# Thirteen small vector loads issued by SyncE behind the first weights, instead of by ScalarE

## What is computed

```python
hn = rmsnorm(h, norm_mix_g[l])      # h is x, (1, 512, 1024)
proj = hn @ w_in[l]                 # (1024, 3592), taken 256 columns at a time
fq, fk, fv, ff, gq, gf, gi, gg = jnp.split(proj, split_idx, axis=-1)
```

## Time and profile before

| | |
|---|---|
| median of 3 runs | 2095.19 us (2094.62 to 2097.42) |
| the profiled execution | 2095.3 us, its span 2093.5 us |
| busy share of the span | PE 97%, VectorE 57%, GpSimd 43%, ScalarE 36% |
| chain that ended last | PE 87%, VectorE 5%, issue 3%, ScalarE 2%, GpSimd 2%, DMA 1% |
| first transpose of x on PE | 5.02 us |
| first matmul of unit 0 | 18.69 us |
| mean granted clock of TensorE | 0.992 |

### The profile page before, as it was taken

How to read it: one execution, slowest core, us unless ns; L and a number is a source line. 1 busy time by engine, 2 the same in 40 slices (tenths; PEclk the granted TensorE clock), 3 DMA queues, 4 the chain that set the end, 5 groups by cost and what they waited for, 6 DMA issues and landing times.

```text
span 2093.5 us, 26082 instructions
## 1 busy us (share of the span) xinstructions
PE 2040.7 (97%) x10286; PEld 1698.6 (81%) x10286; DVE 1197.1 (57%) x1950; ACT 748.8 (36%) x1023; POOL 890.7 (43%) x488
## 2 busy tenths in 40 slices
PE   7999899999999999998999999999999899999998
PEld 6878787888888888876788888888898788888887
DVE  5454656546878895677688766616775763111112
ACT  5344424333513223445643222124353343222221
POOL 3322424654444444444334443443454334444442
PEclk9999999999999999999999999999999999999999
DMA  4322203514455543230146555323332022233321
GB/s 143 106 88 75 76 1 100 159 64 149 137 184 194 179 162 100 81 130 27 41 161 201 174 169 200 119 81 103 101 121 74 31 81 90 96 97 101 101 90 71
DMA packets 225198, 233.39 MB, mean 111 GB/s; under 512 B 4259, under 2 KB 220148, under 8 KB 224956
## 3 DMA queue, kind: packets, MB, share of 16 engines
q1 hardware_dynamic: 224704, 231.70, 34.0%
q10 hardware_dynamic: 380, 0.11, 0.0%
HBM read 229.55 MB, written 2.24 MB: 111 GB/s over the span
## 4 chain that ended last, share of the span: by engine, by line
PE 87%; DVE 5%; issue 3%; ACT 2%; POOL 2%; DMA 1%; ACTq 0%; DVEq 0%; POOLq 0%
PE ps L2329 21%; PE ps L2331 21%; PE ps L2330 21%; PE ps L2380 7%; PE ps L2385 3%; POOL wL L619 2%; PE ps L3156 1%; PE ps L3170 1%; PE ps L2842 1%; DMA raw<-in_w_xkv_dram 1%; PE ps L2773 1%; PE ps L2623 1%; PE ps L2803 1%; DVE ssum L1403 1%; DVE adacc L1866 1%
## 5 line engine op out<-in xcount | busy, mean ns | idle before, releaser
L619 POOL TENSOR_TENSOR wL<-raw,wH 128x1024 fp32r<-128x1024 f32 (+2 forms) x322 | 774.3, 2426 | 1029.5 <-ACT wH L781 969.5
L781 ACT ACTIVATE wH<-raw 128x2048 fp32r<-128x2048 f32 (+2 forms) x161 | 302.4, 1878 | 441.7 <-PE ps L2331 323.9
L2329 PE MATMUL ps<-uH,wH 128*128 128x512 f32 x1088 | 428.2, 394 | 4.7 <-DVE uL L1452 1.9
L2331 PE MATMUL ps<-uH,wL 128*128 128x512 f32 x1088 | 424.7, 390 | 0.0
L2330 PE MATMUL ps<-uL,wH 128*128 128x512 f32 x1088 | 424.1, 390 | 0.0
L2329 PE MATMUL ps<-hnH,wH 128*128 128x512 f32 x728 | 288.8, 397 | 0.0
L2331 PE MATMUL ps<-hnH,wL 128*128 128x512 f32 x728 | 284.1, 390 | 0.0
L2330 PE MATMUL ps<-hnL,wH 128*128 128x512 f32 x728 | 283.4, 389 | 0.0
L1866 DVE SCALAR_TENSOR_TENSOR adacc<-adaw,small,adacc 128x256 f32<-128x256 f32 x336 | 273.5, 814 | 12.0
L2329 PEld LDWEIGHTS ps<-uH,wH 128*128 128x128 f32 x1088 | 204.8, 188 | 49.8 <-issue 4.6
L2331 PEld LDWEIGHTS ps<-uH,wL 128*128 128x128 f32 x1088 | 204.7, 188 | 43.4
(11 more groups left out here) (461 smaller groups left out, 3109.9 us busy)
## 6 DMA issues: line engine op xcount, KB each, us to landing
raw<-in_ffn_w_dram SPq DMA_DIRECT2D x60, 1024.0 KB, 5.3
adaw<-in_ada_w_dram SPq DMA_DIRECT2D x48, 1024.0 KB, 7.3
raw<-in_w_dram SPq DMA_DIRECT2D x32, 1024.0 KB, 5.3
raw<-in_w_in_dram SPq DMA_DIRECT2D x14, 1024.0 KB, 5.4
raw<-in_od_w_in_dram SPq DMA_DIRECT2D x12, 1024.0 KB, 5.3
raw<-in_w_xkv_dram SPq DMA_DIRECT2D x8, 1024.0 KB, 5.7
raw<-in_ffn_w_dram SPq DMA_DIRECT2D x8, 768.0 KB, 4.3
raw<-in_ev_w_in_dram SPq DMA_DIRECT2D x5, 1024.0 KB, 5.2
```

The source lines that it names most:

```text
L619: nc.gpsimd.tensor_tensor(wL[n % 2][:, k0:k1, 0:c], raw[n % 2][:, k0:k1, 0:c], wH[n % 2][:, k0:k1, 0:c].bitcast(F32), ALU.subtract).then_i ...
L781: nc.scalar.activation(wH[n % 2][:, 0:kc, 0:c], raw[n % 2][:, 0:kc, 0:c], ACT.Copy).then_inc(w_hi, 1)
L2329: nc.tensor.matmul(out_ap, wh, xh, start=first, stop=False)
L2331: return nc.tensor.matmul(out_ap, wl, xh, start=False, stop=last)
```

## The change

The first six vector loads (mix, x, memory, feed-forward and final gains, and the lower-bound logits) stay on ScalarE. The other 13 (six rows of the table, four halves of the q and k gains, `ada_b`, `fox_f_bias`, `od_gate_b`) are issued by SyncE, after unit 0 and ahead of the two constant loads and of unit 1. Sources, destinations and the semaphore are the same, and PE waits for all 19 as before. The table of names moved out of ScalarE's program, and the loop's body became `load_vector`.

```diff
+    VECTORS = [("norm_mix_g", V_MIX, 8), ("norm_x_g", V_X, 8), ("norm_mem_g", V_MEM, 8), ("norm_ff_g", V_FF, 8),
+               ("final_norm_g", V_FINAL, 8), ("hgrn_lb_logits", V_LB, 8), ("hgrn_norm_g", V_HG, 1),
+               ("c_2", V_C, 8),
+               ("ev_b_pool_2", V_BPOOL, 4), ("ev_pool_scale_2", V_SPOOL, 4), ("od_conv_w_2", V_CW, 40),
+               ("od_conv_b_2", V_CB, 8)]
+
+    def load_vector(engine, row):
+        name, r0, count = row
+        src = a[name]
+        nd = len(src.shape)
+        flat = {1: "a -> a", 2: "a b -> (a b)", 3: "a b c -> (a b c)"}[nd]
+        src = src if nd == 1 else src.rearrange(flat)
+        return engine.dma_start(vrow[r0:r0 + count, :], src.rearrange("(r m) -> r m", m=P))
@@ -498,6 +512,14 @@
                 sp.dma_start(xtok[:, tb, :], a["x"][0, tb * P:(tb + 1) * P, :]).then_inc(x_in[tb], 16)
             load(0)
+            for row in VECTORS[6:]:
+                load_vector(sp, row).then_inc(vec_in, 16)
+            for name, r0 in (("ev_q_gain_2", V_QG), ("ev_k_gain_2", V_KG)):
+                for half in range(2):
+                    sp.dma_start(vrow[r0:r0 + 1, half * 64:half * 64 + 64], a[name][0:1, :]).then_inc(vec_in, 16)
+            sp.dma_start(brow[0:96, :], a["ada_b_2"].rearrange("l (r m) -> (l r) m", m=P)).then_inc(vec_in, 16)
+            sp.dma_start(fbias[0:8, :], a["fox_f_bias"].rearrange("a b -> b a")).then_inc(vec_in, 16)
+            sp.dma_start(gbias[96:128, :], a["od_gate_b_2"].rearrange("a b -> b a")).then_inc(vec_in, 16)
             sp.dma_start(cst[:, 1:2, :], a["const"][1:2].rearrange("c p m -> p c m")).then_inc(csts_in, 16)
@@ -1013,22 +1035,8 @@
...
-                act.dma_start(vrow[r0:r0 + count, :], src.rearrange("(r m) -> r m", m=P)).then_inc(vec_in, 16)
-            for name, r0 in (("ev_q_gain_2", V_QG), ("ev_k_gain_2", V_KG)):
-                for half in range(2):
-                    act.dma_start(vrow[r0:r0 + 1, half * 64:half * 64 + 64], a[name][0:1, :]).then_inc(vec_in, 16)
-            act.dma_start(brow[0:96, :], a["ada_b_2"].rearrange("l (r m) -> (l r) m", m=P)).then_inc(vec_in, 16)
-            act.dma_start(fbias[0:8, :], a["fox_f_bias"].rearrange("a b -> b a")).then_inc(vec_in, 16)
-            act.dma_start(gbias[96:128, :], a["od_gate_b_2"].rearrange("a b -> b a")).then_inc(vec_in, 16)
+            for row in VECTORS[:6]:
+                load_vector(act, row).then_inc(vec_in, 16)
             act.wait_ge(setup_d, 1)
```

## The result

The changed kernel takes 2100.6 us (median of 20 runs, 2098.11 to 2108.54); the kernel before took 2096.39 us in 20 runs (2094.01 to 2100.26). The ratio is 1.0021 with a 95% interval of 1.0012 to 1.0029, and the medians are 4.2 us apart: slower. The forecast was 2094.9, with a range of 2092.9 to 2096.8. Of the 5.7 us between forecast and result, 1.2 lie in the kernel before, whose median is now 2096.39 and was 2095.19 in three runs.

What follows compares the result with a forecast made beforehand. TensorE's matmuls, busy 97% of the span, bound the kernel, so only the opening's waits counted: a start about 0.5 us earlier, worth 0.4 at the clock, took 2095.3 to 2094.9 us, range 2092.9 to 2096.8.

Steps and rivals of the forecast that it cites:

- part 1: ScalarE's opening: losing 13 issues frees 4.65 us, but the first weights' rounding moves only 1.6 us, waiting for the weights.
- part 2: SyncE's queue: 13 loads behind the first weights are issued until 9.2; vectors land at 12.2 to 13.1, taken as 12.7.
- rival 3: SyncE issues small loads slowly, 0.90 each; first matmul 4.1 us later, 2099.4 and up to 2101; chance 0.04.
- the prediction's own signs: Transposes of vrow after 13.5 mean rival 2 or 3, told apart by SyncE's issue times; before 12, rival 1.
- rival 2: No gain: vectors land at 13.1 or later, or the first low part stalls PE; 2095.3 to 2095.8; chance 0.22.
- part 3: VectorE's root loses 0.40 us of waiting, everything behind keeps its lengths; PE starts at 18.2 in place of 18.69.
- part 5: Later loads cost nothing; VectorE's first low part meets GpSimd's second half, a near tie worth at most 0.2 us.
- part 4: PE's clock: 0.5 us at the start is worth 0.25 if full clock returns unmoved, 0.5 if it moves along; taken 0.4.
- Rival 1: ScalarE's whole gain arrives if vectors land by 11.5: first matmul 1.6 us earlier, at 17.1, worth 0.8 to 1.6; chance 0.10.

Runs made afterwards that it cites:

- e2: Changed kernel with both GpSimd halves of the first unit waiting for VectorE's root: 2098.08 us against 2096.47 before, ratio 1.0007 (0.9997 to 1.0016).
- e7: Changed kernel with 11 of the 13 loads ahead of the first weights on SyncE, the two longest behind: 2103.88 us against 2096.84 before, one run.
- e3: Changed kernel with all 13 loads ahead of the first weights on SyncE: 2095.75 us against 2096.47 before, ratio 0.9998 (0.9988 to 1.0007).
- e8: Changed kernel with 12 loads on ScalarE and 7 on SyncE ahead of the first weights: 2095.11 us against 2096.84 before, ratio 0.9996 (0.9987 to 1.0006).
- e10: Changed kernel with root and broadcast taken ahead of the vectors on VectorE and PE: 2096.24 us against 2096.84 before, ratio 1.0004 (0.9993 to 1.0015).

## Why the prediction was wrong

- **ScalarE (part 1): right.** Table load at 3.15, last square at 9.16, the rounding at 12.33 after 1.69 of waiting for the weights; forecast 3.2, 8.9 and 12.5. Freeing 4.65 us of issues moved the rounding by 1.77.
- **SyncE's issues (part 2): right.** The first took 1.31, the last ended at 9.36; forecast 1.37 and 9.2. An issue took 0.44 on average, under the 0.55 of rival 3. So rival 3, slow issues, did not happen, though its number, a first matmul 4.1 late and 2099.4, is nearly what was measured: the right size from a wrong mechanism. By the prediction's own signs (vectors after 13.5, quick issues) rival 2 came true, late vectors, but it was priced at no more than 2095.8, without what they would meet.
- **The landing of the vectors (part 2): mis-sized, the first error.** Forecast 12.7, at most 13.1; measured 14.16, and 14.0 to 14.6 in the experiments. The bound was taken by bytes from two constant loads for thirteen loads: by size and not by number. The landing read for the first of the two was doubtful as a bound, too: both count on one semaphore. In the changed kernel both stand behind the vectors, and the same reading gives 9.40 + 3.3 = 12.7 for the first, ahead of the vectors' 14.16, and 9.86 + 4.6 = 14.46 for the second. The late end was too early, so the range was too narrow.
- **The root's wait gone (part 3): right**, 0.40. The road behind the vectors is right where nothing meets GpSimd: vectors + 5.5 gives 20.1 in e2 against 20.07. A small slip: the 0.25 between releaser and first matmul is that behind GpSimd; behind ScalarE's rounding it is some 0.13 (21.98 + 0.65 to 22.76).
- **What the earlier GpSimd meets: left out, the second and larger error, 3.2 of 4.1 us.** The step that failed is part 3's "Everything behind it keeps its lengths"; part 5 weighed the lock for the low parts only. By the prediction's figures GpSimd's start moves from 16.07 to about 14.5 and the root's from 13.98 to 13.6, ending at about 14.7, and the two spans were never laid beside each other. They overlap by 0.2, so the root's last instruction would start at about the moment at which GpSimd does. e7 shows what an instruction pays that starts 0.04 behind GpSimd (15.14 against 15.10): 2.32 in place of 0.16, and the next one 2.26. With the vectors at 13.1, the late end of its own bound, the root would start at 14.0 and meet GpSimd for certain, by the same figures. So the forecast of a gain hung on a near tie that it didn't see.
- **The later loads and the clock (parts 4 and 5): the loads hidden, as said.** The second rounding waited for no DMA. At the clock the truth lies between part 4's two cases: in the changed kernel the first matmul is 4.07 later and the end of the half clock 2.06 later (25.80 against 23.74). So the high clock came back neither at the same moment nor in step with the start. The median gaps (4.2, 3.1) agree with the delays of the second unit (3.2, 4.3) within the spread.
- **Rival 1** (the whole gain) needed the vectors by 11.5; e3 and e8 had them at 11.1 and 11.2 and started at 17.8 to 17.9, not at 17.1, as the weights then land later.

## What to carry to other kernels

When an edit makes one engine start earlier, list what every other engine does in the span it now occupies; on VectorE three kinds of instruction of 0.16 us paid the rest of a 2.3 us one of GpSimd, even where they started 0.04 us behind it. Small loads behind a large one cost by their number, so put those that a serial chain waits for ahead of it, or take the chain out of the queue behind them; here either undid the loss at the start (e3, e8, e10), and neither made the kernel measurably faster than before. And before pricing a freed 4.65 us, look for what is second in line: here the weights let the rounding start 1.8 us earlier.

## What was not expected of the hardware

- Thirteen loads, 83 KB, arrive 1.6 to 2.4 us behind the 1 MB ahead of them in the queue; two of them with 136 of the 161 rows arrive 0.5 behind.
- A TENSOR_SCALAR, a TENSOR_TENSOR and a SCALAR_TENSOR_TENSOR on 128x4 elements were each held by a GpSimd TENSOR_TENSOR (1.3 to 2.3 us in place of 0.16 to 0.17); a RECIPROCAL beside it was not (0.18, four runs).
- GpSimd issues a small load in about 0.5 us (0.71 for its first), ScalarE and SyncE in about 0.3; in the changed kernel SyncE's first two behind the 1 MB load took 1.31 and 0.65.
